# Second layer's attention: adding the two halves of the gathered exponentials on the vector engine ahead of the products with ones

## What is computed

```python
s = (jnp.einsum('bqhd,bkhd->bhqk', qn, k_nope)
     + jnp.einsum('bqhr,bkr->bhqk', qr, k_rope)).astype(jnp.float32) * scale
p = jax.nn.softmax(s, axis=-1).astype(v.dtype)
return jnp.einsum('bhqk,bkhd->bqhd', p, v)
```

## Time and profile before

| | us |
|---|---|
| median of 3 runs | 4506.92 (4504.72 to 4507.43) |
| profiled execution | 4512.46 |
| its span | 4510.6 |
| PE busy | 3992.4, 89% of the span |
| DVE busy | 2765.1, 61% |
| ACT busy | 2174.5, 48% |
| POOL busy | 1144.9, 25% |
| granted clock of TensorE, mean | 0.935 |

### The profile page before, as it was taken

How to read it: one execution, slowest core, us unless ns; L and a number is a source line. 1 busy time by engine, 2 the same in 40 slices (tenths; PEclk the granted TensorE clock), 3 DMA queues, 4 the chain that set the end, 5 groups by cost and what they waited for, 6 DMA issues and landing times. The chain is left out here.

```text
span 4510.6 us, 75715 instructions
## 1 busy us (share of the span) xinstructions
PE 3992.4 (89%) x30840; PEld 2784.7 (62%) x30840; DVE 2765.1 (61%) x5076; ACT 2174.5 (48%) x3171; POOL 1144.9 (25%) x919
## 2 busy tenths in 40 slices
PE   7999999758988888887669899797999999999879
PEld 5767767445656556655458687585555555555467
DVE  5556464557768788888565323244676777777433
ACT  4445354586788778787433323122333333333431
POOL 1111111135434343433101000000344444444100
PEclk9999999878989999898679899898999999999989
DMA  4334233311211211211056533465223232322143
GB/s 129 96 106 128 80 109 98 92 38 37 49 33 40 50 40 35 55 41 30 26 177 202 197 127 127 170 222 170 48 64 71 55 80 55 71 65 49 50 165 113
DMA packets 388091, 404.92 MB, mean 90 GB/s; under 512 B 115776, under 2 KB 287488, under 8 KB 387488
## 3 DMA queue, kind: packets, MB, share of 16 engines
q1 hardware_dynamic: 385648, 393.10, 30.3%
q10 hardware_dynamic: 2096, 6.99, 0.4%
HBM read 248.36 MB, written 151.62 MB: 89 GB/s over the span
## 5 line engine op out<-in xcount | busy, mean ns | idle before, releaser
L142 ACT ACTIVATE PT<-psum 128x1024 f32<-128x1024 f32 x384 | 394.2, 1027 | 699.0 <-PE psum L132 695.6
L170 DVE TENSOR_REDUCE m<-psum 128x1 f32<-128x1024 f32 x384 | 467.8, 1221 | 302.3 <-PE psum L132 302.3
L132 PE MATMUL psum<-xc,wah 128*128 128x512 f32 x1600 | 514.6, 403 | 3.2 <-DVE xc L146 2.9
L146 POOL TENSOR_TENSOR part<-PT 128x1024 f32<-128x1024 f32 x144 | 342.0, 2375 | 558.2 <-DVE all L146 381.9
L132 PE MATMUL psum<-PT,V 128*64 128x512 f32 x1536 | 370.3, 603 | 0.0
L143 ACT ACTIVATE bias<-score,cand,cols 128x2048 bf16<-128x2048 f32 (+6 forms) x217 | 314.4, 1449 | 100.9 <-DVE cand L158 97.2
L132 PEld LDWEIGHTS psum<-xc,wah 128*128 128x128 f32 x1600 | 299.7, 190 | 79.4 <-issue 10.3
L143 ACT ACTIVATE sgn<-score,cand,cols 128x1920 bf16<-128x1920 f32 (+6 forms) x217 | 291.1, 1342 | 118.9 <-DVE cand L158 114.4
L146 POOL TENSOR_TENSOR Lm<-gm,cst 64x512 f32<-64x512 f32 x192 | 258.9, 1348 | 302.8 <-PE psum L132 154.0
L132 PE MATMUL psum<-hc,w4h 128*128 128x512 f32 x1024 | 321.0, 395 | 11.3 <-ACT w4h L142 11.3
L132 PE MATMUL psum<-xc,wal 128*128 128x512 f32 x800 | 315.7, 395 | 0.0
(11 more groups left out here) (334 smaller groups left out, 8790.9 us busy)
## 6 DMA issues: line engine op xcount, KB each, us to landing
raw_a<-in_w_a SPq DMA_DIRECT2D x50, 512.0 KB, 4.0
raw_w<-in_w_in SPq DMA_DIRECT2D x32, 512.0 KB, 4.4
QNh<-scr_qnh SPq DMA_DIRECT2D x48, 256.0 KB, 5.2
QRh<-scr_qrh SPq DMA_DIRECT2D x96, 128.0 KB, 5.0
QNl<-scr_qnl SPq DMA_DIRECT2D x48, 256.0 KB, 6.9
xin<-in_x SPq DMA_DIRECT2D x16, 512.0 KB, 4.1
scr_AR<-AR SPq DMA_DIRECT2D x32, 256.0 KB, 2.2
scr_BK<-BK SPq DMA_DIRECT2D x32, 256.0 KB, 2.3
```

What stands on the lines that cost most here:

```text
L132: return self.e.matmul(out, a, b, start=start, stop=stop, skip_group_check=True)
L142: return self.e.activation(out, src, f, bias=bias, scale=scale)
L146: return self.e.tensor_tensor(out, a, b, op) if self.e else self.vector(out)
L170: return self.e.tensor_reduce(out, a, AX, op, negate=negate) if self.e else self.vector(a)
```

## The change

A new entry `half` stands in step 2 of a unit, between the first `max` pass with its `pv`, and the second `max` pass. On DVE it adds the second half of `all` to the first, in place, for both w: two `tensor_tensor` of 128x512 float32 for each unit. `sum` in step 3 then waits for `half`, and has two matmuls where it had four.

```diff
@@ -2649,6 +2649,8 @@
             order_5 += with_row(now[:1])
             if 1 < g < NST + 2:
                 order_5.append(("pv", g // 2 - 1, g % 2))
+            if u and r == 2:
+                order_5.append(("half", u - 1))
             if u and r > 3:
                 order_5.append(("rc", u - 1, r - 4))
             if u and r == 7:
@@ -2819,10 +2821,9 @@
                 elif what == "sum":
                     u = k[1]
                     q.wait_ge(q_dve, "y0", u)
-                    q.wait_ge(q_dve, "acc", 8 * u + 7)
-                    for x in range(2):
-                        for w in range(2):
-                            t = q.mm(bank[6 + u % 2][64 * w:64 * w + 64, :], one[:, 0:64], all5[u % 2][w][:, x, :], x == 0, x == 1)
+                    q.wait_ge(q_dve, "half", u)
+                    for w in range(2):
+                        t = q.mm(bank[6 + u % 2][64 * w:64 * w + 64, :], one[:, 0:64], all5[u % 2][w][:, 0, :])
                     t.then_inc(*q_pe.up("sum", u))
             for k in order_m:
                 what = k[0]
@@ -2924,6 +2925,12 @@
                         if g % 8 > 3:
                             q.wait_ge(q_dve, "acc", g - 2)
                         q.tt(all5[u % 2][w][:, :, :], all5[u % 2][w][:, :, :], part5[w][:, :, :], ALU.add).then_inc(*q_dve.up("acc", g))
+                elif what == "half":
+                    u = k[1]
+                    for w in range(2):
+                        q.wait_ge(q_dve, "acc", 8 * u + 6 + w)
+                        t = q.tt(all5[u % 2][w][:, 0, :], all5[u % 2][w][:, 0, :], all5[u % 2][w][:, 1, :], ALU.add)
+                    t.then_inc(*q_dve.up("half", u))
                 elif what == "fold":
                     u = k[1]
                     q.wait_ge(q_pe, "pv", 4 * u + 3, 1)
```

## The result

The changed kernel takes 4526.76 us (median of 4 runs, 4526.13 to 4528.33), beside 4507.18 us before (4 runs, one more than stood above). The ratio is 1.0044, with a 95% interval of 1.0026 to 1.0061: slower by 19.6 us, where the interval reaches from 12 to 28. The prediction was 4526.3 us, or +19.4.

A forecast was written before the change was run, and what follows sets the result against it. PE alone was taken to bound the attention stage. Stall 1.77 less saving 0.86 gives +0.91 us a unit; 22 units, +20.0, then -0.9 and +0.3, make +19.4 on 4506.9: 4526.3 us, range 4518 to 4532.

The forecast's parts named there:

- The saving: PE's sum in step 3: two matmuls fewer, 2 x 0.43 = 0.86 us for each unit.
- POOL is first, by 0.14 us: Step 2: POOL's addition starts 0.14 us before DVE's first addition could, enough for POOL to be first.
- The block lasts until POOL's end: Step 2: DVE's first addition stands until POOL ends, taking about 2.8 us, to 0.54 behind that end.
- The rival of half speed: Step 2: DVE and POOL share, additions take 2.48 us, stall 0.92 us; 4508 us, chance 0.07.
- The second reduction: Step 2 on DVE, behind the additions: starts at 3618.00 in place of 3615.97, 2.03 us late.
- The stall: PE's look ahead inside step 3's scores waits for the second reduction: 1.66 + 0.11 = 1.77 us a unit.
- The number of units: Units 1 to 22 have the stall, since the look ahead lasts to step 3 of unit 22: 22 x 0.91.
- The sum for the stage: Attention stage: +20.0 for 22 units, -0.9 for unit 23, +0.3 for the last `half`: +19.4 us.
- The clock: PE's granted clock stays at 1.00 despite one 1.8 us stall in some 45 us; nothing charged.
- the first: Step 2: both additions get in ahead of POOL, no stall, only the saving: -19.5, 4487 us, chance 0.08.
- the second: Step 2: only the first addition precedes POOL, stall 0.1 us longer: +21.6, 4528 us, chance 0.05.
- That one wait in PE's queue: Step 3: the look ahead inside the scores waits for step 2's second reduction; PE starts 1.66 us late.

The follow-up runs named there:

- the two kernels without a stall: Edits of the changed kernel: additions moved behind step 2's second reduction, 4490.86 us; or POOL's step 2 addition made to wait for `half`, 4485.82 us.
- the kernel with one input: Changed kernel with four products kept, additions written to an unread tile and their first input read from PSUM: 4507.56 us, ratio 1.0000.
- the kernel with two inputs and four products: Changed kernel with four products kept, additions reading two SBUF inputs and writing to an unread tile: 4546.46 us, ratio 1.0086.

## Why the prediction was right

- **The saving**, 0.86 us a unit. The pieces of PE with four products and with two are 37.29 and 36.41 us: 0.88. In the two kernels without a stall it is the whole of the gain, 0.84 (44.13 - 43.29). Right in size; how it was counted is below.
- **POOL is first, by 0.14 us.** Right: 0.14 in the timeline after. That this lead decides, and not POOL's work as such, is shown by the kernel in which POOL waits; with one input in PSUM the lead doesn't matter.
- **The block lasts until POOL's end.** First addition forecast at about 2.8 us, measured 2.79. The rival of half speed is out: in the stretches of the stage that were read in five of these traces neither is stretched in proportion. A held up DVE instruction of 128x512 ends 0.54 to 0.56 us after POOL, one of 128x1024 1.07 to 1.10, whether it had to stand for 0.3 us or for 2.1, and a held up POOL addition 2.24 to 2.26 after DVE. The page "SBUF — State Buffer" of the Trainium skill says the same in "Who interferes with whom", and also that a DVE instruction with at most one input in SBUF, outside certain modes, doesn't contend; the kernel with one input agrees, with 1.28 us for two additions beside a running POOL.
- **The second reduction** was forecast 0.47 + 0.62 = 1.09 behind POOL's end, PE 1.28 behind the reduction's start. Measured 1.07 (3625.17 - 3624.10) and 1.27 (3626.44 - 3625.17).
- **The stall**, 1.77 us. Shown alone by the kernel with two inputs and four products: 1.77. Net for a unit forecast +0.91, measured 44.13 to 45.02, +0.89.
- **The number of units**, 22. The waits of PE for m are 22.
- **The sum for the stage.** From the fold of unit 1 to the last y of the stage the kernel before has 4217.86 - 3214.66 = 1003.20 us and the changed one 4235.59 - 3213.84 = 1021.75, that is +18.55. Before's trace has the late DMA, and without it the difference would be 0.5 larger, about +19.05. Forecast +19.4. The two profiled spans differ by 15.9 only, since the stages around this one, which the change doesn't touch, happened to be 2.7 us shorter in the second profile. The medians differ by 19.6. That this is within 0.2 us of the forecast is in part luck, since medians of four runs carry an interval of some 8 us each way; what bears the forecast out is the unit, +0.89 against +0.91, and the stage.
- **The clock**, as taken, is the same in both kernels where PE is fed without end: the granted clock is 1.00 in each 100 us from 3300 to 4200 before and after, the upper of the two levels. It is lower only at the stage's end, where PE has gaps in both: 0.94 from 4190 to 4222 before, 0.87 from 4210 to 4240 after.

Of the rivals, the first and the second were each made on purpose and gave what was worked out for them, near 4487 and 4528 us: 4485.82 with DVE first, 4529.41 with only the first addition ahead. That one wait in PE's queue carries the loss was a step of the forecast; moving the waiting pass behind the sum took back 1.32 us of a unit's 1.73.

One step under the sum was wrong, and its number came out right by luck: I took the saving as 0.43 us for each product, two times. It is 0.86 for the pair of products, one for each w, that run side by side, and nothing for an odd one (37.28 us against 37.29). The change happens to remove exactly one such pair.

## What to carry to other kernels

Before work is put into an engine's idle time, look at who else is running in that very gap. A DVE instruction that reads two SBUF tiles and starts behind a POOL addition ends only 0.55 us (128x512) or 1.09 us (128x1024) after POOL's end, and everything behind it in DVE's queue is late by the wait. Where a gap is free of POOL, or POOL can be made to wait for something it isn't in a hurry for, the same work costs nothing: here two small edits turned +0.44% into -0.35% and -0.47%.

Being held up is no loss by itself. In the kernel before, POOL holds up an accumulation of DVE in every unit from 1 to 22, and PE is busy for 100.00 of 100 us all the same, since nothing behind it is late for PE:

```profile
3605.09 2.39 POOL L146 TENSOR_TENSOR all<-PT 128x1024 f32<-128x1024 f32 x1
...
3606.49 2.08 DVE L146 TENSOR_TENSOR all<-all,part 128x1024 f32<-128x1024 f32 x1
```

The row of DVE takes 2.08 us where the same addition takes 1.22 without POOL. What decides is who waits for the next instruction in the queue, and how soon.

## What the runs showed of the hardware that I hadn't expected

DVE lets POOL in between two additions that stand back to back: POOL, starting 0.26 us into the first, did the whole of its 2.38 us of work before the second got on (2.88 us for that one). And float32 products into partitions 0 to 63 and 64 to 127 run side by side at 0.86 us a pair, so that taking away one of an even number saved no time here (37.28 us against 37.29).
